# A k-tile's four matmuls in the experts of a one-core fp32 kernel: high, high, low, low in place of high, low, high, low

## The chip, the cores and the metric

The kernel runs on one core of a Trainium2 chip. The metric is the device time in microseconds of one execution; of the kernel before, three runs gave 3609.1, 3611.16 and 3612.94 us, median 3611.16 us.

## The reference, cut to what matters

One layer of a diffusion backbone: a combined input projection, windowed attention beside a pooling mixer, an output projection, and then sixteen experts, of which each takes its own choice of tokens. The change lies in the experts:

```
def expert_choice_ffn(h, w_router, w_gate, w_up, w_down):
    ...
    cap = EC_FACTOR * xt.shape[0] // N_EXPERTS
    affin = jax.nn.softmax((xt @ w_router).astype(jnp.float32), axis=-1)
    gates, idx = lax.top_k(affin.T, cap)
    xs = xt[idx]
    hid = jax.nn.silu(jnp.einsum('ecd,edf->ecf', xs, w_gate)) * jnp.einsum('ecd,edf->ecf', xs, w_up)
    y = jnp.einsum('ecf,efd->ecd', hid, w_down) * gates[..., None].astype(xt.dtype)
    out = jnp.zeros_like(xt).at[idx.reshape(-1)].add(y.reshape(-1, shp[-1]))
```

The model width is 2048, an expert's inner width 1024. An expert takes 128 tokens of the latent group and 32 of the context group, 160 in all (`CAP`). Everything is float32.

## The kernel before

Each float32 operand is split into a high part, which the fp32r format of TensorE holds, and a low part, the rest. A product is then made of three: high by high, high by low and low by high, all added up in PSUM.

The stages follow each other: the modulation rows and the input projection (to about 900 us), attention and the output projection (to about 1850 us), and the experts, a hardware loop of sixteen turns (1864 to 3528 us), with a short end for the last norm.

In the experts the weights come in pieces of 1 MB: 8 k-tiles of 128 rows by 256 columns. Each expert has 24 of them (`PIECES_E`): for each of four column blocks two of w_gate and two of w_up, and then eight of w_down. SyncE's queue issues the DMA of a piece (line 545) once VectorE has split the piece four places before it. ScalarE copies the piece into `hi_f` (line 1122), VectorE subtracts it from the raw piece into `lo_f` (line 1511), and TensorE waits for `f_lo_ok` once a piece (lines 866 and 882). `hi_f` and `lo_f` have four buffers each.

For a k-tile, `ktile` makes four matmuls. The weights are the stationary operand, in two blocks of 128 columns (`m` = 0 and 1), and the tokens are the moving operand, `x`: 320 columns, of which the first 160 are the tokens' high part and the other 160 their low part. The high weights run over all 320 columns (line 842), the low weights over the first 160 alone (line 844). Block `m` adds into its own PSUM bank, `b + m`. Every matmul has its own weights, so each stands behind a weight load of 128x128 elements.

After the last k-tile of a piece, the last matmul signals `f_used`. On that ScalarE waits before it overwrites the `hi_f` buffer, and before it copies columns 160 to 319 of a finished pair of banks into `part` (lines 1136, 1142, 1154); VectorE adds the other half (lines 1562, 1567, 1590). The next use of the same banks waits for VectorE's sum (`gsum_ok`, `hid_ok`, `yT_ok`), which is made while TensorE works in the other pair of banks. Between pieces of w_down TensorE also turns the next expert's tokens (lines 824 and 826) and this expert's outputs (lines 854 and 856), 40 transposes an expert.

Other streams of matmuls in the kernel serve as rulers. Line 790 (output projection) and line 619 (input projection) run fp32r matmuls of 512 and of 256 moving columns, one weight load each; in both, three matmuls go to one bank and then the bank changes. Line 659 (the router) runs matmuls of 128x128 weights by 16 moving columns.

Of the kernel before, what the change touches and what calls it, by code (L numbers as in the profile page):

```python
# [32 lines left out]
P = 128  # L33
# [150 lines left out]
def hybrid_backbone_step(nc, t, o):  # L184

    ctx = ExitStack()
    with ctx:
# [316 lines left out]
        def mixed_rows(tc, gi):  # L504

            if CH[tc][2] and gi < 3:
                return mix_p[gi], pw_p[gi]
            return pin[:, :, HALO:HALO + CH[tc][1] * P], pw
# [42 lines left out]
        def _(pe):  # L551
# [137 lines left out]
            for tc, (t0, nt, cond) in enumerate(CH):  # L689
# [4 lines left out]
                for k, j in attention_steps(tc):  # L694
                    if k is not None:
# [22 lines left out]
                        else:  # L718
                            gi = 4 * tc + h
                            pe.wait_ge(mixed, gi + 1)  # L720
                            x, w = mixed_rows(tc, h)
# [97 lines left out]
            def turn_tokens(j):  # L819


                for r in range(4):
                    kt = 4 * j + r
                    last = nc.tensor.transpose(PS[:, 4, r * P:(r + 1) * P], g_s[:, kt * P:(kt + 1) * P], ident[:])
                    if j == 0:
                        last = nc.tensor.transpose(PS[:, 5, r * P:(r + 1) * P], g_p[:, r * P:(r + 1) * P], ident[:])
                last.then_inc(x_tr, 1)
# [8 lines left out]
            with pe.Fori(0, NE) as e:  # L836
                def ktile(b, n, r, x, kt, last_kt):


                    for m in range(2):  # L840
                        w = slice(m * P, (m + 1) * P)
                        nc.tensor.matmul(PS[:, b + m, 0:2 * CAP], hi_f[:, n % NSPL_F, r, w], x, start=(kt == 0),  # L842
                                         stop=False, skip_group_check=True)
                        ins = nc.tensor.matmul(PS[:, b + m, 0:CAP], lo_f[:, n % NSPL_F, r, w], x[:, 0:CAP],  # L844
                                               start=False, stop=(kt == last_kt), skip_group_check=True)
                    return ins

                def turn_outputs(cc):

                    pe.wait_ge(yT_ok, e * 8 + 2 * cc + 2)  # L850
                    if cc:
                        pe.wait_ge(ys_ok, e * 4 + cc)
                    for m in range(4):
                        last = nc.tensor.transpose(PS[:, 6, m * P:(m + 1) * P], yT[:, cc % 2, m, :], ident[:])
                        if cc == 3:
                            last = nc.tensor.transpose(PS[:, 7, m * P:(m + 1) * P],
                                                       yTp[:, m].rearrange("p a b -> p (a b)"), ident[:])
                    last.then_inc(y_tr, 1)

                n = 0  # L860
                for q in range(FE // CF):
                    for up in range(2):
                        if q:
                            pe.wait_ge(hid_ok if up else gsum_ok, e * 4 + q)
                        for kg in range(KT // KF):
                            pe.wait_ge(f_lo_ok, e * PIECES_E + NRAW_F + n + 1)
                            for r in range(KF):
                                kt = kg * KF + r
                                if q == 0 and up == 0 and kt % 4 == 0:
                                    pe.wait_ge(x_lo, e * 4 + kt // 4 + 1)  # L870
                                last = ktile(2 * up, n, r, xT[:, kt, :], kt, KT - 1)
                            last.then_inc(f_used, 1)
                            n += 1
                for c in range(D // CF):
                    if c == 0:
                        pe.wait_ge(gsum_ok, e * 4 + 4)
                        pe.wait_ge(hid_lo, e * 4 + 3)
                    elif c == 1:
                        pe.wait_ge(hid_ok, e * 4 + 4)
                    else:  # L880
                        pe.wait_ge(yT_ok, e * 8 + c - 1)
                    pe.wait_ge(f_lo_ok, e * PIECES_E + NRAW_F + n + 1)
                    for r in range(KF):
                        if c == 0 and r == KF - 2:
                            pe.wait_ge(hid_lo, e * 4 + 4)
                        last = ktile(2 * (c % 2), n, r, hid[:, r, :], r, KF - 1)
                    last.then_inc(f_used, 1)
                    n += 1
                    if c % 2 == 0:
                        continue  # L890
                    cc = c // 2
                    if cc == 3:
                        turn_outputs(2)
                    pe.wait_ge(h_in, e * 5 + 7 + cc)
                    pe.wait_ge(x_lo, e * 4 + 4 + cc)
                    turn_tokens(cc)
                    if cc in (1, 2):
                        turn_outputs(cc - 1)
                turn_outputs(3)
# [1053 lines left out]
```

## Time and profile before

| | us |
|---|---|
| median of three runs | 3611.16 |
| profiled execution, its own time | 3611.49 |
| its span, first to last instruction | 3609.7 |
| TensorE matmul busy | 3316.7 (92%) |
| TensorE weight load busy | 3012.9 (83%) |
| VectorE busy | 2137.9 (59%) |
| ScalarE busy | 1752.9 (49%) |
| matmuls, and as many weight loads | 21164 |

The profiled execution's time is 0.33 us over the median of the runs, and 1.8 us lie outside its span.

How to read it: matmuls are pipelined, and the end of a matmul's record is modelled, so the durations of matmuls overlap and their sum is no time. What counts is the spacing from the start of one matmul to the start of the next. A matmul's record starts when it is its turn; if its weights are not in place by then, the wait is part of its record. PE is TensorE's matmuls, PEld its weight loads, DVE VectorE, ACT ScalarE, POOL GpSimd, SP SyncE.

### The profile page before, as it was taken

The page shows a single profiled execution, that of the slowest core. Times are in us where ns is not written, and L with a number is a line of the kernel's source. Part 1 is how long each engine was busy: PE and PEld are TensorE (multiplying, and loading weights), DVE is VectorE, ACT ScalarE, POOL GpSimd, SP SyncE. Part 2 cuts the span into 40 slices and gives each one's busy share as a digit, 9 for nine tenths or more (in the row PEclk, how much of TensorE's full clock was granted, in tenths as well). Part 3 has the DMA queues.
Part 4 walks back from the last instruction along what each step waited for, and adds up shares of the span by engine and source line. Part 5 has one row for each costly group of instructions (what it writes and reads, how often), then busy time and mean ns, then how long its engine had stood idle before and what let it go on. Part 6 is the DMA issues. An engine that isn't in the chain of part 4 may idle for free.

```text
span 3609.7 us, 52586 instructions
## 1 busy us (share of the span) xinstructions
PE 3316.7 (92%) x21164; PEld 3012.9 (83%) x21164; DVE 2137.9 (59%) x2374; ACT 1752.9 (49%) x1820; POOL 570.7 (16%) x611
## 2 busy tenths in 40 slices
PE   5899999999799999998959999999999999999991
PEld 4677777778688877886759999999999999999991
DVE  5634333355342244224977777777777777778774
ACT  5543433365362246224335555555555555555552
POOL 1055035101331013400110000000000000000001
PEclk9999999999799999998979999999999999999995
DMA  7774555577414421442757888888888888888876
GB/s 257 252 246 166 169 182 188 168 256 274 147 30 151 144 100 42 144 148 88 242 193 239 279 271 270 270 264 258 263 265 274 273 273 267 261 266 252 279 227 259
DMA packets 544951, 775.87 MB, mean 215 GB/s; under 512 B 16160, under 2 KB 409600, under 8 KB 536144
## 3 DMA queue, kind: packets, MB, share of 16 engines
q1 hardware_dynamic: 507072, 616.60, 52.3%
q0 software_dynamic: 37776, 157.84, 13.7%
q8 instruction: 72, 1.18, 0.1%
q14 instruction: 31, 0.25, 0.0%
HBM read 708.19 MB, written 66.19 MB: 215 GB/s over the span
## 4 chain that ended last, share of the span: by engine, by line
PE 78%; DVE 7%; ACT 5%; DMA 4%; issue 3%; POOL 2%; ACTq 0%; POOLq 0%; DVEq 0%
PE PS L842 30%; PE PS L619 13%; PE PS L844 12%; PE PS L790 10%; PE PS L736 2%; DVE wlo L1198 2%; PE PS L715 2%; ACT whi L915 1%; PE PS L566 1%; DVE lo_f L1511 1%; PE PS L567 1%; PE PS L724 1%; PE PS L659 1%; PE PS L754 1%; DMA arena_ab<-k_rope 1%
## 5 line engine op out<-in xcount | busy, mean ns | idle before, releaser
L842 PE MATMUL PS<-xT,hi_f 128*128 128x320 f32 x4096 | 1055.1, 346 | 0.0
L1511 DVE TENSOR_TENSOR lo_f<-raw_f,hi_f 128x2048 fp32r<-128x2048 f32 x384 | 878.6, 2288 | 247.9 <-ACT hi_f L1122 246.7
L844 PE MATMUL PS<-xT,lo_f 128*128 128x160 f32 x4096 | 965.9, 236 | 0.0
L1198 DVE TENSOR_TENSOR wlo<-raw,whi 128x2048 fp32r<-128x2048 f32 x204 | 474.9, 2345 | 677.5 <-ACT whi L915 677.1
L844 PEld LDWEIGHTS PS<-xT,lo_f 128*128 128x128 f32 x4096 | 782.3, 191 | 0.0
L1122 ACT ACTIVATE hi_f<-raw_f 128x2048 fp32r<-128x2048 f32 x384 | 733.0, 1909 | 88.8 <-PE PS L844 82.6
L842 PEld LDWEIGHTS PS<-xT,hi_f 128*128 128x128 f32 x4096 | 768.8, 188 | 0.0
L915 ACT ACTIVATE whi<-raw 128x2048 fp32r<-128x2048 f32 x204 | 387.2, 1916 | 550.6 <-PE PS L790 298.8
L842 PE MATMUL PS<-hid,hi_f 128*128 128x320 f32 x2048 | 533.7, 346 | 0.0
L844 PE MATMUL PS<-hid,lo_f 128*128 128x160 f32 x2048 | 482.8, 236 | 0.0
L844 PEld LDWEIGHTS PS<-hid,lo_f 128*128 128x128 f32 x2048 | 390.7, 191 | 0.0
L842 PEld LDWEIGHTS PS<-hid,hi_f 128*128 128x128 f32 x2048 | 384.0, 188 | 0.0
L790 PE MATMUL PS<-whi,ahi 128*128 128x512 f32 x640 | 256.5, 401 | 8.5 <-DVE wlo L1198 8.1
L1883 POOL DMA_INDIRECT resid_s<-y_s,ic_s x16 | 43.2, 2701 | 1372.0 <-DVE y_p L1556 1372.0
L790 PE MATMUL PS<-whi,alo 128*128 128x512 f32 x640 | 252.9, 395 | 0.0
L790 PE MATMUL PS<-wlo,ahi 128*128 128x512 f32 x640 | 252.6, 395 | 0.0
L619 PE MATMUL PS<-whi,ahi 128*128 128x512 f32 x480 | 193.1, 402 | 26.3 <-DVE wlo L1198 13.7
L619 PE MATMUL PS<-whi,alo 128*128 128x512 f32 x480 | 191.4, 399 | 0.0
L619 PE MATMUL PS<-wlo,ahi 128*128 128x512 f32 x480 | 190.8, 397 | 0.0
L566 PE MATMUL PS<-whi,cond_s 128*128 128x512 f32 x384 | 162.3, 423 | 30.7 <-ACT arena_ab L922 16.1
L1154 ACT ACTIVATE part<-PS 128x320 f32<-128x320 f32 x128 | 56.0, 438 | 219.9 <-PE PS L844 219.9
L619 PE MATMUL PS<-ahi,whi 128*128 128x512 f32 (+1 forms) x384 | 140.9, 367 | 17.5 <-DVE wlo L1198 17.5
(266 smaller groups left out, 4619.7 us busy)
## 6 DMA issues: line engine op xcount, KB each, us to landing
raw_f<-w_gate SPq DMA_DIRECT2D x128, 1024.0 KB
raw_f<-w_up SPq DMA_DIRECT2D x128, 1024.0 KB, 5.6
raw_f<-w_down SPq DMA_DIRECT2D x128, 1024.0 KB, 5.4
raw<-w_ada SPq DMA_DIRECT2D x96, 1024.0 KB, 5.2
raw<-w_in SPq DMA_DIRECT2D x60, 1024.0 KB, 5.5
raw<-w_out SPq DMA_DIRECT2D x48, 1024.0 KB, 5.2
arena_ab<-x_sample POOLq DMA_DIRECT2D x8, 1024.0 KB, 12.4
arena_cd<-x_sample POOLq DMA_DIRECT2D x8, 1024.0 KB, 6.8
```

Of the source, the lines that this page charges most:

```text
L566: nc.tensor.matmul(PS[:, 7, :], cond_s[:, kt, :], hi[:, r, :], start=(kt == 0), stop=False)
L619: last = nc.tensor.matmul(out, w, x, start=(kt == 0 and z == 0), stop=(kt == KT - 1 and z == 2))
L715: last = nc.tensor.matmul(flat[:, z * P:(z + n) * P], qTs[b % 2][:, h, :], kT[:, base + kb * P:base + (kb + n) * P], start=True, stop=True ...
L736: last = nc.tensor.matmul(PS[:, 6 + h // 4, (h % 4) * P:(h % 4 + 1) * P], vv[:, kb, (h // 4) * P:(h // 4 + 1) * P], pT[:, slot_of(tc, hc)[ ...
L790: last = nc.tensor.matmul(PS[:, 4 * (cc % 2) + m, :], w, x, start=(first and z == 0), stop=(final and z == 2))
L842: nc.tensor.matmul(PS[:, b + m, 0:2 * CAP], hi_f[:, n % NSPL_F, r, w], x, start=(kt == 0), stop=False, skip_group_check=True)
L844: ins = nc.tensor.matmul(PS[:, b + m, 0:CAP], lo_f[:, n % NSPL_F, r, w], x[:, 0:CAP], start=False, stop=(kt == last_kt), skip_group_check= ...
L915: nc.scalar.activation(whis[slot(n)], raws[slot(n)], ACT.Copy).then_inc(hi_ok, 1)
L1122: nc.scalar.activation(hi_f[:, n % NSPL_F], raw_f[:, n % NRAW_F], ACT.Copy).then_inc(f_hi_ok, 1)
L1154: nc.scalar.activation(part[:, c % 2, :].rearrange("p (a b) -> p a b", a=2), PS[:, b:b + 2, CAP:2 * CAP], ACT.Copy).then_inc(part_ok, 1)
L1198: nc.vector.tensor_tensor(wlos[slot(n)], raws[slot(n)], whis[slot(n)].bitcast(F32), ALU.subtract).then_inc(lo_ok, 1)
L1511: nc.vector.tensor_tensor(lo_f[:, n % NSPL_F], raw_f[:, n % NRAW_F], hi_f[:, n % NSPL_F].bitcast(F32), ALU.subtract).then_inc(f_lo_ok, 1)
```

## The change

In `ktile` the loop over the two column blocks is split in two. Before, the order was high 0, low 0, high 1, low 1; now it is high 0, high 1, low 0, low 1. No matmul, weight load, wait or signal is added or taken away; the last matmul, which carries the signal, is the same one, low 1. Each bank gets its additions in the same order as before.

```diff
@@ -841,6 +841,8 @@
                         w = slice(m * P, (m + 1) * P)
                         nc.tensor.matmul(PS[:, b + m, 0:2 * CAP], hi_f[:, n % NSPL_F, r, w], x, start=(kt == 0),
                                          stop=False, skip_group_check=True)
+                    for m in range(2):
+                        w = slice(m * P, (m + 1) * P)
                         ins = nc.tensor.matmul(PS[:, b + m, 0:CAP], lo_f[:, n % NSPL_F, r, w], x[:, 0:CAP],
                                                start=False, stop=(kt == last_kt), skip_group_check=True)
                     return ins
```

## Rows read from the trace of the kernel before

**Rows 1.** The page: granted clock in forty slices, and the chain that ended last.

```profile
PEclk9999999999799999998979999999999999999995
...
PE 78%; DVE 7%; ACT 5%; DMA 4%; issue 3%; POOL 2%; ACTq 0%; POOLq 0%; DVEq 0%
```

**Rows 2.** Windows over eight experts: engines' busy time, granted clock, DMA.

```profile
core 0: us, PE busy (x) PEld busy (x) DVE busy (x) ACT busy (x) POOL busy (x), PEclk, DMA share, GB/s
1970.00:2386.00 416.00, 411.72 (x3232) 410.88 (x3231) 316.05 (x320) 237.99 (x221) 30.92 (x16) 1.00 0.85 267
2386.00:2802.00 416.00, 411.72 (x3232) 410.89 (x3230) 315.94 (x321) 237.99 (x221) 31.28 (x16) 1.00 0.85 267
```

**Rows 3.** Waits of TensorE from 1970 to 3218 us, twelve experts.

```profile
engine line waited for: us in total, times, longest us
PE PS L854 <- DVE y_s L1553: 11.8, 11, 1.1
```

**Rows 4.** Timeline within a w_gate piece: start us, us, engine, line, tiles.

```profile
2699.96 0.34 PE L842 MATMUL PS<-xT,hi_f 128*128 128x320 f32 x1
2699.99 0.19 PEld L844 LDWEIGHTS PS<-xT,lo_f 128*128 128x128 f32 x1
2700.14 0.24 PE L844 MATMUL PS<-xT,lo_f 128*128 128x160 f32 x1
2700.14 0.19 PEld L842 LDWEIGHTS PS<-xT,hi_f 128*128 128x128 f32 x1
2700.21 0.35 PE L842 MATMUL PS<-xT,hi_f 128*128 128x320 f32 x1
...
2700.25 0.19 PEld L844 LDWEIGHTS PS<-xT,lo_f 128*128 128x128 f32 x1
2700.40 0.23 PE L844 MATMUL PS<-xT,lo_f 128*128 128x160 f32 x1
2700.40 0.19 PEld L842 LDWEIGHTS PS<-xT,hi_f 128*128 128x128 f32 x1
2700.47 0.34 PE L842 MATMUL PS<-xT,hi_f 128*128 128x320 f32 x1
```

**Rows 5.** Experts' matmuls by line: count, min/median/max ns, first to last start us.

```profile
L842 PE MATMUL PS<-xT,hi_f x235: 342/346/348, 1974.8 to 2034.9; 128*128 128x320 f32 x118
...
L844 PE MATMUL PS<-xT,lo_f x234: 232/237/238, 1975.0 to 2034.8; 128*128 128x160 f32 x117
```

**Rows 6.** The same view of line 790 (1597 to 1624 us) and line 619.

```profile
L790 PE MATMUL PS<-whi,alo x41: 389/389/389, 1596.8 to 1624.0; 128*128 128x512 f32 x41
...
L619 PE MATMUL PS<-alo,whi x31: 283/283/283, 873.4 to 884.2; 128*128 128x256 f32 x31
```

**Rows 7.** The same view of line 659, the router, 1276 to 1279.4 us.

```profile
L659 PE MATMUL PS<-wra,arena_cd x32: 177/262/263, 1275.9 to 1279.3; 128*128 128x16 f32 x32
```

**Rows 8.** Timeline of eight transposes; line 824 writes bank 4, line 826 bank 5.

```profile
2044.12 0.27 PE L824 MATMUL PS<-ident,g_s 128*128 128x128 f32 x1
2044.23 0.27 PE L826 MATMUL PS<-ident,g_p 128*128 128x128 f32 x1
...
2044.88 0.27 PE L826 MATMUL PS<-ident,g_p 128*128 128x128 f32 x1
```

**Rows 9.** VectorE's splits by line and DMA's rate in slices, 1970 to 3218 us.

```profile
L1511 DVE TENSOR_TENSOR lo_f<-raw_f,hi_f 128x2048 fp32r<-128x2048 f32 x288 | 658.9, 2288 | 182.4 <-ACT hi_f L1122 181.5 <-issue 0.8
...
GB/s 279 293 245 237 316 249 232 306 274 241 280 294 244 235 313 252 231 299 284 238 283 291 246 230 315 253 234 303 279 237 283 290 248 230 310 256 235 299 285 236
```

## The prediction

> **What bounds the kernel now.** I read the chain that ended last first, then the experts' stretch in windows, then who keeps TensorE waiting there, and then the single matmuls. The chain belongs to TensorE for 78% [rows 1]. In the experts it is nearly all of it: over eight experts TensorE is busy 411.7 us in each 416, at granted clock 1.00, which is the 2.4 GHz level, while VectorE is busy 316 us, ScalarE 238 us and the DMA engines for 0.85 [rows 2]. The only wait of TensorE that the trace names in twelve experts is one of 1.1 us an expert, before the last transposes of the outputs [rows 3]. An expert takes 416 / 4 = 104.0 us with 3232 / 4 = 808 matmuls: 24 pieces of 8 k-tiles of 4 matmuls, which is 768, and 40 transposes. So the time of the experts is the spacing of these matmuls, and the reader should look at starts, not at durations.
>
> **The spacing of today.** Line 842 starts 235 times from 1974.8 to 2034.9 us [rows 5]: 60.1 us / 234 = 257 ns for a pair of one high matmul (320 columns) and one low matmul (160 columns). The sum for an expert is 384 pairs x 257 ns = 98.7 us, 40 transposes x 0.109 us [rows 8] = 4.4 us and the wait of 1.1 us: 104.2 us, against 104.0.
>
> What would a pair cost if only its columns counted? Two rulers: fp32r matmuls of 512 columns, each with its own weight load, follow each other at 27.2 us / 40 / 3 = 226.7 ns, and those of 256 columns at 10.8 us / 30 / 3 = 120.0 ns [rows 6]. The line through both is 0.417 ns a column and 13.3 ns a matmul. It gives 146.7 ns for 320 columns and 80.0 ns for 160, together 226.7 ns. The pair takes 257 ns, so some 30 ns of each pair are not columns.
>
> Where do they lie? By the rulers' durations (389 and 283 ns, 0.414 ns a column, [rows 6]) the record of a 320-column matmul should be 283 + 64 x 0.414 = 309.5 ns; it is 346. The 160-column one should be 243 and is 237 [rows 5]. The high matmul carries 36 ns of waiting, the low one none. The starts say the same: after the start of a low matmul the next high one is due at once, 70 ns later, while the next weight load starts 30 to 40 ns late after it and at once after the low one [rows 4]. I read it so: one set of weights can be loaded behind the running matmul and no more. The load of the low weights runs behind the 147 ns of a high matmul and is hidden. The load of the high weights can start only as the low matmul starts, takes longer than the low matmul's 80 ns, and the next high matmul waits for it. 257.0 less 146.7 leaves 110.3 ns for the load's slot.
>
> Is 110 ns a load's price elsewhere? In the router the moving operand has 16 columns, which by the line is 20 ns, and yet 32 of these matmuls start from 1275.9 to 1279.3 us, 109.7 ns apart [rows 7]. That is a stream in which every matmul waits for its weights. The transposes follow at 0.76 us / 7 = 108.6 ns [rows 8]. So the rule that I take is: the spacing from one matmul to the next is the larger of the first one's columns (0.417 ns each and 13.3 ns) and the next one's weight load (109 to 111 ns).
>
> **The change, part by part.** Nothing is removed or added: the same four matmuls and four loads a k-tile, the same waits once a piece, the same signal on the same last matmul, so nobody's buffer comes free earlier or later in a piece but through the spacing. It moves one high matmul ahead of one low one. Before, a k-tile had the transitions high to low, low to high, high to low, low to high: 2 x 257.0 = 514.0 ns. After, it has high to high, high to low, low to low, low to high. The second and the last of these are as today, 257.0 ns together. New are two:
> - high to high: 320 columns run while a load of 110 ns runs behind them, so 146.7 ns. The ends: 146.7, and 148 to 150, since the starts alone split the pair a little otherwise (the low matmul starts 180 to 190 ns after the high one, of which 36 ns are the high one's waiting [rows 4, 5]).
> - low to low: 160 columns (80 ns) run while a load of 110 ns runs behind them, so the load decides. The router's stream is the nearest row, since both neighbours there wait as well: from 108.6 (the transposes [rows 8]) to 112.9 (the router's, with the view's rounding: 3.5 us / 31 [rows 7]). I take 110.3, what the same weights cost today.
>
> The sum: 257.0 + 146.7 + 110.3 = 514.0 ns a k-tile, as before. There are 16 experts x 24 pieces x 8 = 3072 k-tiles. At the low ends the two new transitions take 255.3 ns, 1.7 less than today, and the rounding of today's 257.0 (0.1 us / 234, twice a k-tile) adds 0.9: 2.6 x 3072 = 8 us faster. At one of the upper ends they take 3.3 or 2.6 ns more: 8 to 10 us slower; both at once I leave out as unlikely. The reader should see why the order does not matter: as long as every load costs the same and each hides only behind the one matmul before it, two high matmuls hide two loads and two low ones fail to hide two, in either order.
>
> Three further things, each costed at nothing. Banks: today every second matmul changes its PSUM bank, after the change every one does. In lines 790 and 619 one of three changes it and the spacing stays 226.7 and 120.0 [rows 6], and transposes that change it each time run at 108.6 [rows 8], so a change of bank shows no price. The wait of 1.1 us an expert [rows 3] comes from VectorE behind the last piece, and the piece ends with the same matmul. The other engines are covered by TensorE and stay so at an unchanged spacing; if it fell, VectorE has 316 of 416 us to do [rows 2], 2288 ns of split for a piece of 16 x 257 = 4118 ns, and DMA has slices at 316 GB/s against its mean of 267 [rows 9], so a gain of a few per cent would come through.
>
> **Weighed against the Trainium skill.** The rows show a load's slot of 109 to 111 ns. The Trainium skill, "TensorE: Matmul & The Clock Gate", section "LDWEIGHTS (loading the stationary operand)", puts a load at its columns over 1.2 GHz, 107 ns for 128, which agrees; its section "Back-to-back issue gap" speaks against it, with 81 ns for a sustained stream of loads and matmuls of 128 columns. By that figure a low to low transition would cost some 81 ns and the change would gain.
>
> **The rivals.**
> Faster: the 30 ns are not the load's time but belong to the step from a low matmul to a high one, say because a matmul of a new length or from the other tile of weights is set up late. Then they are paid twice a k-tile today and once after the change, and low to low costs 80 ns: (110.3 - 80) x 3072 = 93 us, 3611 - 93 = 3518 us. For it: in the experts this wait is seen only at that step. Against it: the router's matmuls, all of one length and from one tile, are 109.7 ns apart [rows 7]. Chance 0.10.
>
> Slower: a weight load behind a matmul that has itself waited starts late. In the timeline the low weights' load is recorded 30 to 40 ns after the high matmul that waited, where the high weights' load is recorded within 10 ns of the low one that did not [rows 4]. Today that delay lies behind 147 ns of columns. After the change the second low matmul has waited, lasts 80 ns, and the next high weights load behind it: if the 34 ns came on top of the 110.3, each k-tile would lose 34 ns, 104 us in all, 3715 us. It decides as soon as the waiting matmul is shorter than 34 + 110 ns. Against it: in the router each matmul waits and lasts 20 ns, and the spacing is 109.7, not 144 [rows 7]; the delay in the record is then the wait itself, as I read it. Chance 0.07.
>
> That the change does not do what it says: the page counts as many loads as matmuls, so no load is shared or dropped today, and in both orders each matmul's weights differ from those before. I give it nothing.
>
> **How the numbers follow.** The sum is made against the profiled execution, 3611.5 us, which is 0.3 us over the median; so the forecast is 3611 us, with chance 0.83. Its own range is -8 to +10 us, widened by the 2 us that the runs lie about their median: 3601 to 3623 us. Within it I give 0.74 to a difference of up to 0.2% (7 us, about what a measurement of this kernel can tell from no change), 0.04 to the low end beyond it and 0.05 to the high end. With the rivals: faster 0.14, same 0.74, slower 0.12. The rivals lie 93 and 104 us away, each with a chance of at most 0.10; the range does not reach to either and leaves out 0.17.
>
> **What would show it right or wrong.** In the new timeline a k-tile still takes 514 ns, the period of an expert is 104.0 us, and 235 starts of line 842 still span some 60 us. Of line 842's records half stay at 346 ns (the first of a k-tile, behind a low matmul) and half fall to some 310; of line 844's half stay at 237 ns and half rise to some 273. If all of line 844's are near 237 and the k-tile takes 484 ns, the faster rival holds; if the k-tile takes 548 ns with line 842's first record near 380, the slower one. The prediction is also wrong if TensorE's waits in the experts are no longer the 1.1 us alone, or if the granted clock leaves 1.00.

## The result and the profile after

The changed kernel takes 3627.03 us (median of 7 runs, 3621.79 to 3639.54); the kernel before takes 3605.2 us over 7 runs. The ratio is 1.0062, with a 95% interval from 1.0044 to 1.0081: slower, by 16 to 29 us (22 by the medians). I had forecast no change, 3611 us, with 3601 to 3623 us as the range.

The loss is in the experts. Source view of lines 842 and 846 (846 is the low matmul's line now): count, min/median/max ns, first to last start in us.

```profile
L842 PE MATMUL PS<-xT,hi_f x4096: 305/347/615, 1874.1 to 3520.3; 128*128 128x320 f32 x196
...
L846 PE MATMUL PS<-hid,lo_f x2048: 235/255/278, 1942.3 to 3556.2; 128*128 128x160 f32 x187
```

From the first matmul of the experts to the last it is 3556.2 - 1874.1 = 1682.1 us; before it was 1663.7 (from the same view, 1864.5 to 3528.2). That is 18.4 us more. The profiled execution took 3639.54 us, its span 3637.7, which is 28.0 more than the span before; the other 9.6 us lie ahead of the experts (they start at 1874.1 in place of 1864.5), where nothing is changed. The start of the experts moved between 1848 and 1874 us from one profile to the next in all the kernels below, so I take no meaning from it. The experts' own stretch is steadier: it takes 1663.3 to 1664.7 us in all five profiles, here and below, of kernels with the same matmul lengths at 513.3 ns a k-tile, and 1681.1 to 1682.2 us in all four of such kernels mostly at 520.0. Of the 22 us between the medians it accounts for 18; the rest lies within what the runs of one kernel differ by.

Windows over what were eight experts show the same picture as [rows 2], with fewer matmuls done:

```profile
core 0: us, PE busy (x) PEld busy (x) DVE busy (x) ACT busy (x) POOL busy (x), PEclk, DMA share, GB/s
1970.00:2386.00 416.00, 411.75 (x3194) 410.91 (x3194) 313.06 (x315) 235.23 (x217) 32.59 (x16) 1.00 0.85 265
```

TensorE is as busy as before, at granted clock 1.00, and gets through 3194 matmuls in place of 3232. Its waits are those of [rows 3]:

```profile
PE PS L856 <- DVE y_s L1555: 12.8, 12, 1.1
```

So it is the spacing. One row over a long stretch of gate and up pieces, the counterpart of [rows 5]:

```profile
L842 PE MATMUL PS<-xT,hi_f x233: 305/348/393, 2401.6 to 2462.0; 128*128 128x320 f32 x117
```

232 high matmuls after the first are 116 k-tiles: 60.4 / 116 = 0.521 us a k-tile, where it was 0.514. The timeline of TensorE in w_down pieces shows more. It merges two neighbours of one kind into one row (x2). First two pieces, 20 and 21 of the sixth expert (12 k-tiles lie between the first and the last of these rows), then pieces 22 and 23 (14 k-tiles):

```profile
2488.08 0.49 PE L842 MATMUL PS<-hid,hi_f 128*128 128x320 f32 x2
2488.41 0.35 PE L846 MATMUL PS<-hid,lo_f 128*128 128x160 f32 x2
...
2494.24 0.49 PE L842 MATMUL PS<-hid,hi_f 128*128 128x320 f32 x2
...
2496.12 0.50 PE L842 MATMUL PS<-hid,hi_f 128*128 128x320 f32 x2
2496.46 0.35 PE L846 MATMUL PS<-hid,lo_f 128*128 128x160 f32 x2
...
2503.40 0.50 PE L842 MATMUL PS<-hid,hi_f 128*128 128x320 f32 x2
```

6.16 us / 12 = 513.3 ns and 7.28 us / 14 = 520.0 ns. The same matmuls, on the same tiles' buffers, run at two speeds, each of them steady. I worked out every k-tile's time in this way from the starts in the trace. Behind the first k-tiles of a piece, the changed kernel has 520.0 ns in 22 of the 24 pieces of each expert and 513.3 ns in pieces 20 and 21, in all sixteen experts. The kernel before has 513.3 ns in all pieces but for the first k-tiles behind a wait (its k-tiles are mostly 512 and 515 ns in turn, 1026.7 for two). In the mean of all, 519.4 against 513.5: 5.9 ns x 3072 k-tiles = 18.3 us. That is the 18.4 us.

The source view for both kinds of pieces gives the parts of the step, min/median/max. High and low of pieces 20 and 21, then of pieces 22 and 23:

```profile
L842 PE MATMUL PS<-hid,hi_f x24: 305/327/349, 2488.1 to 2493.9; 128*128 128x320 f32 x24
...
L846 PE MATMUL PS<-hid,lo_f x22: 235/255/275, 2488.4 to 2493.6; 128*128 128x160 f32 x22
...
L842 PE MATMUL PS<-hid,hi_f x24: 312/330/348, 2496.8 to 2502.9; 128*128 128x320 f32 x24
...
L846 PE MATMUL PS<-hid,lo_f x24: 237/254/272, 2497.0 to 2502.8; 128*128 128x160 f32 x24
```

The first high matmul and the second low one carry the wait for weights (348 and 272 ns), as predicted; the second high matmul (305 or 312) and the first low one (235 or 237) carry none. Between the two rhythms it is chiefly the second high matmul, which waits for nothing, that grows: by 7 ns in its record. The starts say where the time goes. From the first high matmul to the second, to the first low, to the second low and to the next k-tile they are 187, 143, 74 and 110 ns apart in the fast rhythm (sixth expert, piece 21) and 187, 149, 76 and 108 ns in the slow one (piece 4): nearly all of the 6.7 ns stands between the second high matmul and the first low one.

### The profile page after: what moved, and what is told of

Its sections match the earlier page's. It is cut to its first block, busy times and chain, and to the rows that moved or that the text cites. A ratio compares the mean times of both kernels' runs of the same rounds, so it can differ in the third digit from the quotient of the medians.

```text
span 3637.7 us, 52586 instructions
## 1 busy us (share of the span) xinstructions
PE 3345.3 (92%) x21164; PEld 3039.5 (84%) x21164; DVE 2139.3 (59%) x2374; ACT 1753.1 (48%) x1820; POOL 575.4 (16%) x611
## 4 chain that ended last, share of the span: by engine, by line
PE 80%; DVE 7%; ACT 4%; DMA 4%; issue 3%; POOL 2%; ACTq 0%; POOLq 0%; DVEq 0%
PE PS L842 28%; PE PS L846 16%; PE PS L619 13%; PE PS L790 11%; PE PS L736 2%; DVE wlo L1200 2%; PE PS L715 2%; ACT whi L917 1%; PE PS L566 1%; PE PS L659 1%; PE PS L567 1%; PE PS L724 1%; PE PS L754 1%; DMA arena_ab<-k_rope 1%; DMA raw<-w_ada 1%
## 5 line engine op out<-in xcount | busy, mean ns | idle before, releaser
L842 PE MATMUL PS<-xT,hi_f 128*128 128x320 f32 x4096 | 1022.8, 330 | 0.0
L846 PE MATMUL PS<-xT,lo_f 128*128 128x160 f32 x4096 | 712.9, 255 | 0.0
L846 PEld LDWEIGHTS PS<-xT,lo_f 128*128 128x128 f32 x4096 | 691.2, 188 | 0.0
L842 PEld LDWEIGHTS PS<-xT,hi_f 128*128 128x128 f32 x4096 | 622.7, 192 | 0.0
L842 PE MATMUL PS<-hid,hi_f 128*128 128x320 f32 x2048 | 510.8, 330 | 0.0
L846 PE MATMUL PS<-hid,lo_f 128*128 128x160 f32 x2048 | 356.5, 255 | 0.0
L846 PEld LDWEIGHTS PS<-hid,lo_f 128*128 128x128 f32 x2048 | 343.4, 188 | 0.0
L842 PEld LDWEIGHTS PS<-hid,hi_f 128*128 128x128 f32 x2048 | 310.7, 192 | 0.0
L567 PE MATMUL PS<-wlo,cond_s 128*128 128x512 f32 x384 | 156.7, 408 | 0.0
```

The costliest lines, as they stand in the source:

```text
L567: last = nc.tensor.matmul(PS[:, 7, :], cond_s[:, kt, :], lo[:, r, :], start=False, stop=(kt == KT - 1))
```

## The experiments

I started from three theories. A: a change of PSUM bank costs some 3 ns, and the change has four of them in a k-tile in place of two. B: two long matmuls and then two short ones can fall into a slower rhythm, which the start of a stretch picks. C: two loads in a row out of the same tile of weights cost more. Where times per k-tile are given, they are means over the k-tiles behind the first three of each piece, from the starts in the trace. Single runs of one kernel differ by some 20 us (the kernel before from 3594.6 to 3616.9 us), so k-tile times decide below, and the total only where it was timed in rounds.

**Swapped high matmuls.** The lengths of the changed kernel with two bank changes a k-tile.

```diff
-                    for m in range(2):
+                    for m in (1, 0):
                         w = slice(m * P, (m + 1) * P)
                         nc.tensor.matmul(PS[:, b + m, 0:2 * CAP], hi_f[:, n % NSPL_F, r, w], x, start=(kt == 0),
```

> Order high 1, high 0, low 0, low 1: lengths as in the changed kernel (two long, two short), but only two bank changes a k-tile, as in the kernel before. Nothing is left out. Theory A (a change of PSUM bank costs some 3 ns, and the changed kernel has four of them in place of two): a k-tile goes back from 520 to 513 or 514 ns, and the time from 3627 to about 3607 us. Theory B (two long matmuls and then two short ones fall into a slower rhythm, whatever the banks): most k-tiles stay at 520 ns, some 3627 us.

Measured: 520.0 ns a k-tile in the same 22 pieces, 513.7 in pieces 20 and 21 (513.3 in fifteen experts, and 520.0 in the first one, with the same instructions). Time 3621.97 us against 3607.04, ratio 1.0052 (1.0033 to 1.0071). Source view of line 842:

```profile
L842 PE MATMUL PS<-xT,hi_f x233: 309/312/348, 2381.8 to 2442.1; 128*128 128x320 f32 x117
```

60.3 / 116 = 0.520 us. Halving the bank changes gave nothing back.

**The old order with a bank change at every matmul.** All high matmuls add into bank b, all low ones into b + 1.

```diff
-                        nc.tensor.matmul(PS[:, b + m, 0:2 * CAP], hi_f[:, n % NSPL_F, r, w], x, start=(kt == 0),
+                        nc.tensor.matmul(PS[:, b, 0:2 * CAP], hi_f[:, n % NSPL_F, r, w], x, start=(kt == 0 and m == 0),
...
-                        ins = nc.tensor.matmul(PS[:, b + m, 0:CAP], lo_f[:, n % NSPL_F, r, w], x[:, 0:CAP],
-                                               start=False, stop=(kt == last_kt), skip_group_check=True)
+                        ins = nc.tensor.matmul(PS[:, b + 1, 0:CAP], lo_f[:, n % NSPL_F, r, w], x[:, 0:CAP],
+                                               start=(kt == 0 and m == 0), stop=(kt == last_kt), skip_group_check=True)
```

> The order before (long, short, long, short), but all high matmuls add into bank b and all low ones into bank b+1, so the bank changes at every matmul. The experts' sums are no longer those of the reference; the work is the same. Theory A: 520 ns a k-tile, some 3625 us. Theory B: 513 or 514 ns, 3605 to 3611 us.

Measured: 513.3 ns in every piece, 3597.9 us in one run. The row:

```profile
L842 PE MATMUL PS<-xT,hi_f x236: 342/346/348, 2373.8 to 2434.1; 128*128 128x320 f32 x118
```

60.3 / 235 x 2 = 0.513 us. With both runs theory A falls.

**Lengths alone and tiles alone.** In both kernels the four matmuls are written out as z = 0 to 3. In the first the lengths are 320, 320, 160, 160 and the weights high, low, high, low; in the second the lengths are 320, 160, 320, 160 and the weights high, high, low, low.

```diff
+                    for z in range(4):
+                        m, c = z // 2, (2 * CAP, CAP)[z // 2]
+                        w = slice(m * P, (m + 1) * P)
+                        ins = nc.tensor.matmul(PS[:, b + z % 2, 0:c], (hi_f, lo_f)[z % 2][:, n % NSPL_F, r, w], x[:, 0:c],
...
+                        m, c = z % 2, (2 * CAP, CAP)[z % 2]
...
+                        ins = nc.tensor.matmul(PS[:, b + z // 2, 0:c], (hi_f, lo_f)[z // 2][:, n % NSPL_F, r, w], x[:, 0:c],
...
```

> Lengths as in the changed kernel (320, 320, 160, 160 columns), weights as in the kernel before (high, low, high, low), the bank changes at every matmul. The second and third matmul take the wrong number of columns, so the sums differ from the reference. Theory B (lengths): most pieces at 520 ns a k-tile. Theory C (two loads in a row from the same tile of weights cost more): 513 ns everywhere.

> The reverse: lengths alternate (320, 160, 320, 160) as in the kernel before, weights as in the changed kernel (high, high, low, low). The sums differ from the reference in the same way. Theory B: 513 ns everywhere, some 3600 to 3611 us. Theory C: most pieces at 520 ns.

Measured: lengths alone 520.0 ns in 22 pieces and 513.8 in pieces 20 and 21 (again 520.0 in the first expert and 513.3 in the others), the pattern of the changed kernel; tiles alone 513.3 ns in every piece. Rows of the first kernel, then of the second:

```profile
L843 PE MATMUL PS<-xT,hi_f x233: 235/348/393, 2385.9 to 2446.3; 128*128 128x320 f32 x117
```

```profile
L843 PE MATMUL PS<-xT,lo_f x235: 232/342/347, 2377.8 to 2437.8; 128*128 128x320 f32 x118
```

60.4 / 116 = 0.521 us and 60.0 / 117 = 0.513 us. Theory C falls; what counts is the sequence of lengths.

**Shifted starts.** One more matmul ahead of each of an expert's 16 groups (a group starts where `kt` is 0), in the changed order and in the old one.

```diff
+                    if kt == 0:
+                        c = 232 + 4 * (n // 2 if n < 16 else n - 8)
+                        nc.tensor.matmul(PS[:, b, 0:c], hi_f[:, n % NSPL_F, r, 0:P], x[:, 0:c], start=True,
+                                         stop=True, skip_group_check=True)
```

> The changed order, with one more matmul ahead of each of the 16 groups of an expert, overwritten by the next one: 232, 236, ... 292 columns, so that the groups start shifted against each other by 1.7 ns each. Theory B with two rhythms that the start picks: some groups run at 520 ns a k-tile and some at 513, and which ones goes with the number of columns, the same in every expert. Theory A, or a fixed price for a transition: all groups at 520 ns. The 256 added matmuls cost 110 to 135 ns each, some 30 us in all.

> The order before, with the same 16 added matmuls an expert. If the slow rhythm belongs to the order high, high, low, low alone: every group at 512 to 515 ns a k-tile, whatever the start, and the time some 30 us over the kernel before. If the old order has a slow rhythm too and was only lucky in its starts: some groups at 520 ns.

Measured: in the changed order 11 of the 24 pieces now run at 513.3 to 513.8 ns and 13 at 519.6 to 520.0; a piece keeps its rhythm in all sixteen experts, but for pieces 18 and 20 in the first one. The groups behind 236, 240, 252, 256, 260 and 272 columns are the fast ones. In the old order all 24 pieces stay at 513.3 ns. The times of the single runs were 3657.8 and 3643.4 us. From the first to the last matmul the experts took 1705.1 and 1695.6 us, 9.5 us apart. The means, 516.9 and 513.3 ns, would make 11 us of it over 3072 k-tiles, somewhat too much, since the first k-tile of a group takes the same in both. Two groups of the changed order, behind 232 and 240 columns:

```profile
2404.47 0.50 PE L846 MATMUL PS<-xT,hi_f 128*128 128x320 f32 x2
...
2411.23 0.50 PE L846 MATMUL PS<-xT,hi_f 128*128 128x320 f32 x2
...
2420.07 0.31 PE L842 MATMUL PS<-xT,hi_f 128*128 128x240 f32 x1
...
2420.70 0.49 PE L846 MATMUL PS<-xT,hi_f 128*128 128x320 f32 x2
...
2427.89 0.49 PE L846 MATMUL PS<-xT,hi_f 128*128 128x320 f32 x2
```

6.76 / 13 = 0.520 us and 7.19 / 14 = 0.5136 us a k-tile, for the same instructions. Neighbouring groups differ by four columns, 1.7 ns, and by what ran before them; that is enough to pick the rhythm, and it then holds for the group's k-tiles.

**First k-tile in the old order.** A start shifted at no cost, with the changed order everywhere else.

```diff
-                    for m in range(2):
+                    order = ((0, 0), (1, 0), (0, 1), (1, 1)) if kt == 0 else ((0, 0), (0, 1), (1, 0), (1, 1))
+                    for low, m in order:
```

> The changed kernel, but the first k-tile of each of an expert's 16 groups in the old order (high, low, high, low) and the other 152 of 192 in the new one, or 176 of them; nothing is left out. By the transitions it costs the same. Theory B (the start picks the rhythm): groups now start shifted, and some or all of the pieces that ran at 520 ns run at 513; if all, 3605 to 3610 us, as fast as before. If the new order has a fixed price: the new-order k-tiles stay at 520 ns, some 3624 us.

Measured (176 of an expert's 192 k-tiles are in the changed order): the pieces settle at 520.0 ns, 20 and 21 now too. A group of the sixth expert, piece 2, goes 514, 516, 517 and then 520 ns five times. Time 3622.79 us against 3608.91, ratio 1.0044 (1.0025 to 1.0064). The start matters, since the two fast pieces were lost, but I steered the wrong way: from here the slow rhythm is where it settles. This run alone would also fit a price that comes up after some k-tiles; the shifted starts exclude it as fixed.

**Blocks of four.** Two k-tiles together: four high matmuls, then four low ones.

```diff
-                    for m in range(2):
-                        w = slice(m * P, (m + 1) * P)
-                        nc.tensor.matmul(PS[:, b + m, 0:2 * CAP], hi_f[:, n % NSPL_F, r, w], x, start=(kt == 0),
-                                         stop=False, skip_group_check=True)
+                    for z in range(2):
+                        for m in range(2):
+                            w = slice(m * P, (m + 1) * P)
+                            nc.tensor.matmul(PS[:, b + m, 0:2 * CAP], hi_f[:, n % NSPL_F, r + z, w], x[z],
+                                             start=(kt + z == 0), stop=False, skip_group_check=True)
...
-                            for r in range(KF):
+                            for r in range(0, KF, 2):
```

The low matmuls are looped in the same way.

> Two k-tiles together: four high matmuls, then four low ones. Nothing is left out. My rule of the prediction gives 1026.7 ns for two k-tiles, as for any order. Theory B (what costs is that long ones and short ones stand in pairs, once a k-tile): as the step from the one kind to the other comes once in two k-tiles, at most 6.7 ns more, 1033 ns. If each pair of neighbours of one kind costs, there are six in place of four in two k-tiles and the loss grows to 20 ns, 1047 ns, some 31 us over the kernel before in all.

> The kernel of blocks of four again (four high matmuls, then four low ones; nothing left out), now timed against the kernel before. Its k-tiles ran at 513.3 ns. If the 6.7 ns a k-tile are the whole of what the changed kernel lost, this order, which moves the matmuls further than the change does, costs nothing: ratio 1.000, with 1.002 at most. If moving matmuls costs something besides the rhythm: 1.004 or more.

Measured: 1026.7 ns for two k-tiles, 513.3 each, in every piece. Timed in five rounds, 3607.56 us against 3606.7, ratio 1.0001 (0.9988 to 1.0014). A row of the timed run:

```profile
L843 PE MATMUL PS<-xT,hi_f x236: 302/308/393, 2385.7 to 2445.7; 128*128 128x320 f32 x118
```

The order that moves the matmuls furthest has three neighbours long to long and three short to short in two k-tiles, and costs nothing. No price belongs to these transitions as such, and without the slow rhythm nothing is lost.

**A ruler.** From the second k-tile on all four matmuls have 128 + 8n columns in piece n.

```diff
+                    c = 128 + 8 * n
+                    ch, cl = (c, c) if kt else (2 * CAP, CAP)
```

The high matmuls then take `0:ch` and the low ones `0:cl`.

> A ruler: from the second k-tile on, all four matmuls of a k-tile have the same number of columns, 128 + 8n in piece n of an expert (128 to 312). Only those columns are added up, so the experts' sums are not the reference's. If a matmul costs the larger of 0.417 ns a column + 13.3 ns and a load of 110 ns: 110 ns flat up to 232 columns, then a straight line to 143.3 ns at 312. If starts fall on a raster (6.7 ns fits 513.3 and 520 ns a k-tile), the k-tile's time climbs in steps of 6.7 ns or so, not straight.

Measured, ns a k-tile at the 2.4 GHz level: 446.7 flat from 128 to 232 columns and 447.9 at 240; then 460.0 (248 columns), 480.0 (256), 480.0 (264), 506.7 (272), 510.6 (280), 526.7 (288), 542.9 (296), 552.3 (304), 571.7 (312). Two parts are left out. Piece 8 (192 columns) ran mostly at the 1.2 GHz level (its stretch has granted clock 0.76) after a wait of TensorE for VectorE; its last k-tiles are back at 447 ns in most experts. And pieces 0 to 7 of the first expert ran at that level throughout, at 853 ns a k-tile, as this window of them shows (granted clock 0.50):

```profile
1860.00:1900.00 40.00, 40.00 (x188) 40.00 (x187) 15.18 (x12) 14.58 (x13) 1.89 (x2) 0.50 0.55 186
```

The kernel before has 0.50 in the first 2.5 us of its experts and 1.00 from 4.5 us on. Timeline at 256 and at 264 columns:

```profile
2457.90 0.40 PE L844 MATMUL PS<-hid,hi_f 128*128 128x256 f32 x2
...
2460.30 0.40 PE L844 MATMUL PS<-hid,hi_f 128*128 128x256 f32 x2
...
2461.79 0.40 PE L844 MATMUL PS<-hid,hi_f 128*128 128x264 f32 x2
...
2464.19 0.40 PE L844 MATMUL PS<-hid,hi_f 128*128 128x264 f32 x2
```

2.40 us for five k-tiles in both. The load's floor of 111.7 ns a matmul is confirmed (I had 110.3). The line of the rulers is not a law: 264 columns cost 120.0 ns and not 123.3, 280 cost 127.7 and not 130. The climb has steps, of which several are 6.7 ns a k-tile or a multiple (460.0, 480.0, 506.7, 526.7), but not all (510.6, 542.9, 552.3, 571.7). Those four are means of k-tiles that differ among themselves; the last part of the next section comes back to them.

**The short length, scanned.** The low matmuls take 96 + 8n columns in piece n, from the second k-tile on, in the changed order and in the old.

```diff
+                    c = 96 + 8 * n if kt else CAP
...
-                        ins = nc.tensor.matmul(PS[:, b + m, 0:CAP], lo_f[:, n % NSPL_F, r, w], x[:, 0:CAP],
+                        ins = nc.tensor.matmul(PS[:, b + m, 0:c], lo_f[:, n % NSPL_F, r, w], x[:, 0:c],
```

> The changed order, but from the second k-tile on the low matmuls have 96 + 8n columns in piece n (96 to 280) in place of 160; the sums differ from the reference. My rule (load 111 ns, line of the rulers): about 514 ns a k-tile up to 232 columns, then rising to 2 x (146.7 + 130) = 553 ns at 280. If the slow rhythm needs two matmuls in a row that wait for their loads: times over the rule only up to some 232 columns, and none above. If it needs only pairs of unlike lengths: over the rule on both sides.

> The same columns in the old order. My rule gives the same times as for the run before. Theory B: 513 ns up to 232 columns throughout, with none at 520, and the paired order never faster than this one.

Measured, ns a k-tile, for half of the lengths and without the first expert, whose first pieces ran at the 1.2 GHz level (960 ns a k-tile at 104 columns, granted clock 0.50):

| columns | changed order | old order |
|---|---|---|
| 104 | 514.2 | 520.0 |
| 112 | 520.0 | 513.4 |
| 128 | 520.0 | 520.6 |
| 152 | 513.4 | 516.6 |
| 160 | 513.4 | 513.4 |
| 184 | 520.0 | 513.2 |
| 208 | 513.3 | 513.3 |
| 216 | 513.3 | 520.0 |
| 232 | 513.3 | 521.9 |
| 256 | 533.3 | 533.2 |
| 264 | 533.3 | 543.6 |
| 272 | 546.7 | 540.0 |

Timeline of the old order at 104 columns, 14 pairs apart:

```profile
2389.09 0.38 PE L843 MATMUL PS<-xT,hi_f 128*128 128x320 f32 x1
...
2392.73 0.38 PE L843 MATMUL PS<-xT,hi_f 128*128 128x320 f32 x1
```

3.64 / 14 x 2 = 520 ns. My expectation that the old order has no slow rhythm fails: it holds at 160 columns, but the old order has 520 ns at 104, 144 and 216. Up to 232 columns both orders lie between 513 and 522 ns, some lengths in between the two values, and which order is ahead changes with the length. In the changed order no length above 232 columns is over my rule, as it would be if the slow rhythm needed two matmuls in a row that wait; but in the old order no two such stand in a row, so that is not its condition. At 256 columns, where no load is waited for, both have 533.3, the sum of the rulers (2 x 146.7 + 2 x 120.0). The changed order with 160 columns ran at 513.4 here, where each group starts behind another length; that is one more sign that the start decides.

## Why the prediction was wrong

What held. The experts are TensorE's alone, at granted clock 1.00, with the same single wait. The 30 ns of a pair are the wait of a matmul for its weights behind a short one: the ruler's floor is 111.7 ns for any length from 128 to 232 columns; and after the change the first high and the second low matmul carry the wait (348 and 272 ns), the other two do not, as the last part of the prediction had it. The bank change costs nothing. The Trainium skill, "TensorE: Matmul & The Clock Gate", section "Back-to-back issue gap", gives 81 ns for a stream of loads and matmuls of 128 columns; the ruler has 111.7 ns at 128 columns, so for these fp32r operands the measurement decides against it. Neither rival came: the gain of 93 us did not show, and the delay of 34 ns behind a waiting matmul did not add up.

What failed is the step "The sum: 257.0 + 146.7 + 110.3 = 514.0 ns a k-tile". It takes a k-tile as four independent prices, one for each transition. The sum names only the faster of two rhythms (513.3 ns). In the other, the same four matmuls take 520.0 ns, and the changed kernel spends 22 of 24 pieces in it. The term that was missing is 6.7 ns a k-tile; it is not the price of a neighbour, since blocks of four have more such neighbours and lack it, nor of a bank or a tile. A better price of a load does not mend the sum either: with the ruler's 111.7 ns it gives 2 x (146.7 + 111.7) = 516.8 ns, which is neither rhythm.

The size was within my own ends, but by luck. I had 148 to 150 ns for high to high and up to 112.9 for low to low, and both together give +5.9 ns and 18 us, the number that was measured; I cut the range to one of the two at a time, as "both at once I leave out as unlikely". With 18 us kept it would have reached 3631 us and held the result. The time does not lie where those ends put it, though. From the first high start to the second it is 187 ns in both rhythms, and from the first low start to the end of the second low record it is 348 to 349 ns in both (74 + 275, 76 + 272). What grows is the spacing from the second high matmul to the first low one, 143 to 149 ns, a transition that I had taken "as today".

The profile had given a hint that I did not use: line 842's records in [rows 5] run from 342 to 348 ns and line 844's from 232 to 238, where the single-length streams of [rows 6] have 389 and 283 at minimum, median and maximum alike. The mixed sequence of lengths was hunting between neighbouring values, and these two pure ones were not. That is no property of pure streams: the later ruler, with one length throughout, hunts too at some lengths (at 280 columns its k-tiles go 514, 509, 510 ns, and again). The two lengths on which my line rests happened to be steady ones.

I also wrote that a gain of a few per cent would come through. The ruler casts doubt on that. At the 2.4 GHz level its k-tiles take 472 ns in the mean of the 24 pieces in place of 513; over the 2816 k-tiles with the new lengths that is 116 us, but the experts took 1659.0 us in place of 1663.7. TensorE now waits for VectorE's sum (line 1566) once an expert:

```profile
PE PS L844 <- DVE gsum L1566: 42.7, 12, 3.7
```

42.7 / 12 = 3.6 us an expert, 57 us in sixteen. The k-tiles at the 1.2 GHz level took another 52 us (22 in the first expert, 30 in piece 8, right behind these waits). Both together are nearly all that the shorter matmuls had saved. It is no clean test of a small gain, since the ruler makes pieces 0 to 7 faster by 13%.

What stays open is what the rhythms are. Times that differ by 6.7 ns a k-tile, steady for up to 141 k-tiles in a row and picked by a few nanoseconds in the start, look like starts that fall on a raster. The traces bear that out further. Where the spacings within a piece repeat after one, two or three k-tiles, at the 2.4 GHz level, one repetition takes a whole number of 6.667 ns, as well as records in whole nanoseconds can tell: 513.3 and 520.0 ns (77 and 78), the 1026.7 for two k-tiles of the kernel before (154), the ruler's 446.7, 460.0, 480.0, 506.7 and 526.7 (67, 69, 72, 76, 79). The ruler's 510.6 and 552.3 belong here too: at 280 columns three k-tiles take 1533.3 ns and repeat (230 steps), at 304 columns 1653.3 (248 steps). At 240, 296 and 312 columns a piece shows no repetition. No run here shows what the raster would belong to. Nor did I find which start leads where: only that the groups behind 236 and 240 added columns ran at 513.3 and those behind 232 and 244 at 520.0. No order was found that beats the kernel before; blocks of four equal it.

## What to carry to other kernels

Where matmuls of unlike lengths alternate and some wait for their weights, a sum of transitions gives the time of a sequence to about 1.3% and no better (513.3 or 520.0 ns here for the same work), so a reordering that is free by the sum should be measured before it is kept. When spacings are read for a loop, look for the sum over the whole period, piece by piece, not only for medians: two steady values in one kernel are a sign that the start may pick the rhythm, which shifted starts can show. And a range should not leave out that two terms of one pattern are off together, unless a row shows that they are independent.

## What I had not expected of the hardware

The same instructions on the same buffers have two steady speeds, 513.3 and 520.0 ns a k-tile, and the start decides between them: the group behind 240 added columns is fast, the next one, behind 244, is slow (its start is set by the group before it as well). An fp32r matmul of 264 columns costs no more than one of 256 (120.0 ns each), and one of 128 no less than one of 232 (111.7 ns), each with its own weight load. The start-to-start pattern, where it repeats, takes a whole number of 6.667 ns in all these kernels.
